# GpSimd rounds and subtracts the weight chunks up to the mixing weights in eight pieces each in place of four

## The chip, the cores and the metric

The kernel runs on one core of a Trainium2 chip. The metric is the device time of one launch in microseconds (us); lower is better. Before the change it is 1716.6 us, the median of three runs (1716.49 to 1716.98).

## What is computed

One decoder layer in float32 on a sequence of 1024 tokens with 1024 features: an input projection; for eight heads, sparse attention in which an indexer picks 256 keys for each query; for eight more heads, attention in a window of 128 tokens with learned sinks; an output projection; cross-attention into 256 memory tokens; an MLP of width 4096 with squared ReLU; a layer norm after each of the three parts.

```python
proj = h @ w_in[l] + b_in[l]
o_dsa = dsa_sparse_attention(dq, dk, dv, iq, ik, iw)      # top-256 keys by an indexer's score
o_swa = swa_sink_attention(sq, sk, sv, swa_sinks[l])
mix = jnp.concatenate([o_dsa, o_swa], axis=-1) @ w_o[l]
h = layer_norm(DEEPNORM_ALPHA * h + mix, ln1_g[l], ln1_b[l])
c = memory_cross_attention(h, mem, wq_mem[l], wk_mem[l], wv_mem[l], wo_mem[l])
h = layer_norm(DEEPNORM_ALPHA * h + c, ln2_g[l], ln2_b[l])
m = squared_relu_mlp(h, w_up[l], w_down[l])
h = layer_norm(DEEPNORM_ALPHA * h + m, ln3_g[l], ln3_b[l])
```

## The kernel before, in words

**Split products.** TensorE multiplies numbers of the type fp32r, which keeps fewer bits than float32. To lose nothing the kernel splits every operand into a rounded part (`hi`) and the rest (`lo`), and each product is three matmuls: hi times hi, hi times lo, lo times hi (`exact`, L584 to L586).

**Weight chunks.** All weights come as 68 chunks of 128 partitions by 2048 columns (chunk 0 has 1600 columns). Their order is fixed: 0 for the values and the indexer's weights (`C_V`), 1 for the keys, 2 to 7 for the queries, 8 to 23 for the four memory heads (four chunks a head: wk, wv, wq, wo), 24 to 27 for the mixing weights w_o, 28 to 35 for the two products of the cross-attention, 36 to 67 for the MLP. `C_MIX` is 24 and `C_G` is 28. SyncE (SP) loads a chunk into one of two buffers `raw`. GpSimd (POOL) then runs two passes over it: L570 rounds (`w_hi`, one input), L575 subtracts (`w_lo`, two inputs). Each pass is cut into `PIECES` instructions of equal width, four of 512 columns, with all rounding ahead of all subtracting. Each subtraction adds one to the semaphore `w_ready`. TensorE waits until all pieces of the chunk that it needs are counted, and SP until all pieces of the chunk two back are counted; nobody waits for a single piece. Up to chunk 23 there are two buffers for the split weights, so POOL starts a chunk once TensorE has used the chunk two back (`chunk_used`).

**The start.** VectorE (DVE) makes the angles for the rotary tables (L1114 to L1126, 1024 columns each, every one waiting for the one before), and then the lo parts of x (`x_lo`, L1130, eight of 1024 columns). ScalarE (ACT) rounds x (L864) and evaluates sine and cosine in between. TensorE's first matmul waits for chunk 0 and for the first `x_lo`.

**The middle.** TensorE projects the queries and keys (`project`), computes the indexer's scores, and then walks through the attention units, windowed heads first, with one product of the memory heads' weights (`memory_product`) put in after about every third unit of these. VectorE evacuates logits (L1465) and meanwhile finds each query's 256 best keys by a search over the bits of a threshold (`select_keys`): a counting pass over the scores (L1245, 384 to 768 columns), then three instructions of one to three columns each that take the bit back or keep it (L1287, L1293, L1299). ScalarE counts for the two widest tiles, and VectorE evaluates these counts (`set_wide`: L1378, L1383, L1389, L1397). All this is written in one fixed order for each engine.

**The rest.** From the last attention units on, TensorE has products to do almost without a break: mixing, cross-attention, MLP.

Of the kernel before, what the change touches and what calls it, by code (L numbers as in the profile page):

```python
# [55 lines left out]

V_COLS = HEADS + HEAD + 2 * HEAD
CHUNK = 2048
PIECES = 4
C_V, C_K, C_IQ, C_SQ, C_DQ = 0, 1, 2, 4, 6  # L60
C_MEM = 8
C_MIX = C_MEM + 4 * MEM_HEADS
C_G = C_MIX + 4
C_U = C_G + 4
C_MLP = C_U + 4
N_FF = FF // 256
N_CHUNKS = C_MLP + 2 * N_FF

TWO_PI = 2.0 * np.pi

# [119 lines left out]
def build_layer(nc, a):  # L190
# [6 lines left out]
    with ctx:  # L197
        def sem(name):
            return ctx.enter_context(nc.semaphore(name))
# [181 lines left out]
        w_rounded = sem("w_rounded")  # L381
        w_ready = sem("w_ready")
# [40 lines left out]
        def columns_of(c):  # L423
            return NK * V_COLS if c == C_V else CHUNK
# [21 lines left out]
        def _(sp):  # L446
# [58 lines left out]
            att_loaded = 3  # L505
            for c in range(2, N_CHUNKS):
                if c == C_DQ:
                    load_keys()
                    for j in range(NT - FIRST_TOPK_TILE):
                        load_queries(j)  # L510
                if c == C_MEM:
                    for j in range(3):
                        load_queries(NT - FIRST_TOPK_TILE + j)
                if c == C_MEM + 2:

                    chunk_used(sp, C_MEM - 1)
                    sp.dma_start(mem_raw[:], a["mem_t"]).then_inc(mem_in, 16)

                if C_MEM + 2 < c <= C_MIX + 2:
                    ahead = 2 * NT if c == C_MIX + 2 else 3 + (mem_unit(c - 3) - 1) // HEADS  # L520
                    while att_loaded < ahead:
                        load_queries(NT - FIRST_TOPK_TILE + att_loaded)
                        att_loaded += 1
                if c == C_MIX + 2:

                    chunk_used(sp, C_MIX - 1)
                    for s in range(2):
                        sp.wait_ge(stored[s], 16 * 4 * MEM_HEADS)

                    attended(sp, 2 * NT - 1)  # L530
                    load_gb(0)
                if c == C_U + 1:

                    sp.wait_ge(ln_done, NT)
                    load_gb(1)
                if c == C_MLP + 2:

                    sp.wait_ge(ln_done, 2 * NT)
                    load_gb(2)

                sp.wait_ge(w_ready, PIECES * (c - 1))
                dst = raw[c % 2][:, 0:columns_of(c)]
                if C_G <= c < C_MLP:
                    dst = dst.rearrange("p (k n) -> p k n", k=4)
                sp.dma_start(dst, source_of(c)).then_inc(raw_in[c % 2], 16)
# [7 lines left out]
        @block.gpsimd  # L553
        def _(pool):
            for c in range(N_CHUNKS):
                s, n = slot_of(c), columns_of(c)

                pool.wait_ge(raw_in[c % 2], 16 * (c // 2 + 1))

                if 2 <= c < C_MIX + 2:  # L560
                    chunk_used(pool, c - 2)
                elif C_MIX + 2 <= c < C_MIX + 4:

                    attended(pool, 2 * NT - 1)
                elif c >= C_MIX + 4:
                    chunk_used(pool, c - 4)

                for p in range(PIECES):
                    col = slice(p * n // PIECES, (p + 1) * n // PIECES)
                    pool.tensor_scalar(w_hi[s][:, col], raw[c % 2][:, col], 1.0, 1.0, ALU.mult, ALU.mult)\  # L570
                        .then_inc(w_rounded, 1)
                for p in range(PIECES):
                    col = slice(p * n // PIECES, (p + 1) * n // PIECES)
                    pool.wait_ge(w_rounded, PIECES * c + p + 1)
                    pool.tensor_tensor(w_lo[s][:, col], raw[c % 2][:, col], w_hi[s][:, col].bitcast(F32),  # L575
                                       ALU.subtract).then_inc(w_ready, 1)

# [2 lines left out]
        def _(pe):  # L580
# [11 lines left out]
                return [w[s][:, 0:n].rearrange("p (k n) -> p k n", k=k) for w in (w_hi, w_lo)]  # L592


            pe.wait_ge(w_ready, PIECES * (C_V + 1))
            wh, wl = parts_of(C_V, NK)
            for k in range(NK):
                pe.wait_ge(x_lo_done, k + 1)
# [7 lines left out]
            def project(r, j):  # L606

                c, _, hf = ROPE[r]
                n = A_ROPE + 2 * r + j
                if n == 0:  # L610

                    pe.wait_ge(v_done, 2)
                if r == N_ROPE_FIRST and j == 0:

                    indexed(pe, i_free, len(IDX) - 4)
                pe.wait_ge(w_ready, PIECES * (c + 1))
                freed(pe, a_free, n)
                wh, wl = parts_of(c, NK)
                col = slice(j * P, (j + 1) * P)
                tok = slice(hf * HALF, (hf + 1) * HALF)  # L620
                exact(ring_a[n % 2][:], [(wh[:, k, col], wl[:, k, col], x_hi[:, k, tok], x_lo[:, k, tok])
                                         for k in range(NK)]).then_inc(a_full[n % 2], 1)
# [30 lines left out]
            def memory_product(use):  # L653


                h, what = divmod(use, 10)
                n = A_MEM + 10 * h
                m = n + what
                if use == 0:
                    pe.wait_ge(mem_lo_done, 1)  # L660
                pe.wait_ge(w_ready, PIECES * (C_MEM + 4 * h + (what if what < 2 else 2 + (what - 2) // 4) + 1))
                freed(pe, a_free, m)
                dst = ring_a[m % 2]
                if what < 2:
                    wh, wl = parts_of(C_MEM + 4 * h + what, NK)
                    for j in range(2):
                        col = slice(j * P, (j + 1) * P)
                        mm = exact(dst[:, j * MEM:(j + 1) * MEM],
                                   [(wh[:, k, col], wl[:, k, col], mem_hi[:, k, :], mem_lo[:, k, :])
                                    for k in range(NK)])  # L670
                elif what < 6:

                    emptied(pe, a_free, n)
                    wh, wl = parts_of(C_MEM + 4 * h + 2, 2)
                    for j in range(2):
                        col = slice((2 * (what - 2) + j) * P, (2 * (what - 2) + j + 1) * P)
                        mm = exact(dst[:, j * MEM:(j + 1) * MEM],
                                   [(wh[:, k, col], wl[:, k, col], kv_hi[0][:, k, :], kv_lo[0][:, k, :])
                                    for k in range(2)])
                else:  # L680

                    emptied(pe, a_free, n + 1)
                    wh, wl = parts_of(C_MEM + 4 * h + 3, 2)
                    mt, half = divmod(what - 6, 2)
                    row = slice(mt * P, (mt + 1) * P)
                    col = slice(half * HALF, (half + 1) * HALF)
                    mm = exact(dst[:], [(kv_hi[1][:, k, row], kv_lo[1][:, k, row], wh[:, k, col], wl[:, k, col])
                                        for k in range(2)])
                mm.then_inc(a_full[m % 2], 1)
# [89 lines left out]
            def product(g):  # L779

                stage, ch, t = g // (2 * NT), g // NT % 2, g % NT
                n = L_GEMM + g
                c = C_MIX + 4 * stage + 2 * ch
                pe.wait_ge(w_ready, PIECES * (c + 2))
                act_split(stage, t)
                freed(pe, l_free, n)
                for kh in range(2):
                    wh, wl = parts_of(c + kh, 4)
                    mm = exact(ring_l[n % 2][:, 0:HALF],
                               [(act_hi[:, t, 4 * kh + k, :], act_lo[:, t, 4 * kh + k, :],  # L790
                                 wh[:, k, :], wl[:, k, :]) for k in range(4)],
                               first=(kh == 0), final=(kh == 1))
                mm.then_inc(l_full[n % 2], 1)

            def up(u):

                f, hf = divmod(u, 2)
                wh, wl = parts_of(C_MLP + 2 * f, NK)
                pe.wait_ge(w_ready, PIECES * (C_MLP + 2 * f + 1))
                if f == 0:  # L800
                    for t in range(4 * hf, 4 * hf + 4):
                        act_split(3, t)
                for j in range(2):
                    n = A_UP + 2 * u + j
                    freed(pe, a_free, n)
                    col = slice(j * P, (j + 1) * P)
# [5 lines left out]
            def down(u):  # L812

                f = u // 2
                wh, wl = parts_of(C_MLP + 2 * f + 1, 2)
                pe.wait_ge(w_ready, PIECES * (C_MLP + 2 * f + 2))

                pe.wait_ge(hid_ready, 2 * u + 2)
                for tt in range(4):
                    n = L_DOWN + 4 * u + tt  # L820
                    freed(pe, l_free, n)
                    tok = slice(tt * P, (tt + 1) * P)
                    for half in range(2):
                        col = slice(half * HALF, (half + 1) * HALF)
# [912 lines left out]
```

## Time and profile before

| | us |
|---|---|
| median of 3 runs | 1716.6 |
| the profiled execution's own time | 1712.85 |
| its span, first instruction to last | 1711.1 |
| TensorE busy | 1546.0 (90%) |
| VectorE busy | 965.3 (56%) |
| GpSimd busy | 551.4 (32%) |
| ScalarE busy | 443.5 (26%) |

The chain of waits that ended last is 72% TensorE, 19% VectorE, 3% ScalarE and 2% GpSimd; 4% is issue. Busy time includes the time in which an instruction has begun and is held up, so a short instruction with a long duration is one that waited inside its engine.

### The profile page before, as it was taken

To read this page: it belongs to the slowest core of one execution; us is meant where nothing else is said; L and a number is where in the kernel's file an instruction comes from. 1 tells how busy PE (TensorE), PEld (TensorE's weight loads), DVE (VectorE), ACT (ScalarE), POOL (GpSimd) and SP (SyncE) were. 2 spreads that over 40 slices of the span, in tenths; PEclk is the share of its full clock that TensorE was granted. 3 is DMA by queue.
4 is the path that set the end of the run, shared out by engine and by line. 5 is a ranking of instruction groups with operands and counts; after the bars stand their busy time and mean duration, and the time that the engine had idled before them with its cause. 6 is when DMAs were issued, how large, how long until landed. Compare 5 with 4: busy or idle time off the path is not lost.

```text
span 1711.1 us, 20895 instructions
## 1 busy us (share of the span) xinstructions
PE 1546.0 (90%) x7720; PEld 1305.8 (76%) x7720; DVE 965.3 (56%) x1819; ACT 443.5 (26%) x961; POOL 551.4 (32%) x548
## 2 busy tenths in 40 slices
PE   5997884688787999998999999999999999999993
PEld 5885663678686998877888778888888888888882
DVE  5568998799987443277442943333333333333348
ACT  2015334455544764112220111111111111111110
POOL 5341031364462000334333053333333333333100
PEclk9999997788886999999999999999999999999997
DMA  5463043243431102222110041111111111110002
GB/s 214 136 204 129 25 154 129 80 137 130 148 123 46 42 2 87 93 93 74 50 50 1 1 148 49 50 50 50 50 50 49 50 49 50 49 50 25 1 1 98
DMA packets 61332, 128.97 MB, mean 75 GB/s; under 512 B 6960, under 2 KB 34096, under 8 KB 53552
## 3 DMA queue, kind: packets, MB, share of 16 engines
q1 hardware_dynamic: 44208, 100.37, 17.5%
q10 hardware_dynamic: 17024, 27.27, 4.5%
q8 instruction: 62, 1.02, 0.2%
q14 instruction: 38, 0.31, 0.1%
HBM read 100.35 MB, written 27.26 MB: 75 GB/s over the span
## 4 chain that ended last, share of the span: by engine, by line
PE 72%; DVE 19%; issue 4%; ACT 3%; POOL 2%; ACTq 0%; DMA 0%; DVEq 0%; SPq 0%; POOLq 0%
PE banks L584 21%; PE banks L586 21%; PE banks L585 21%; PE banks L741 4%; DVE unread L1245 3%; PE banks L719 2%; DVE score L1216 2%; DVE h_buf L1546 1%; PE banks L751 1%; PE banks L633 1%; DVE bn L1532 1%; PE banks L634 1%; POOL w_lo L575 1%; ACT unread_wide L908 1%; DVE trial L1293 1%
## 5 line engine op out<-in xcount | busy, mean ns | idle before, releaser
L570 POOL TENSOR_SCALAR w_hi<-raw 128x512 fp32r<-128x512 f32 (+1 forms) x272 | 181.4, 693 | 1059.1 <-PE banks L586 770.2
L575 POOL TENSOR_TENSOR w_lo<-raw,w_hi 128x512 fp32r<-128x512 f32 (+1 forms) x272 | 372.5, 1400 | 0.0
L1657 DVE TENSOR_TENSOR h_buf<-h_buf,banks 128x1024 f32<-128x1024 f32 x120 | 146.4, 1220 | 146.6 <-PE banks L586 146.6
L584 PE MATMUL banks<-w_hi,hid_hi 128*128 128x512 f32 x512 | 200.8, 392 | 7.8 <-DVE h_buf L1657 7.8
L584 PE MATMUL banks<-act_hi,w_hi 128*128 128x512 f32 x512 | 200.1, 391 | 1.7 <-DVE act_lo L1525 1.7
L586 PE MATMUL banks<-w_hi,hid_lo 128*128 128x512 f32 x512 | 200.4, 391 | 0.0
L585 PE MATMUL banks<-w_lo,hid_hi 128*128 128x512 f32 x512 | 200.4, 391 | 0.0
L586 PE MATMUL banks<-act_hi,w_lo 128*128 128x512 f32 x512 | 199.9, 390 | 0.0
L585 PE MATMUL banks<-act_lo,w_hi 128*128 128x512 f32 x512 | 199.7, 390 | 0.0
L1621 DVE TENSOR_TENSOR relu_buf<-relu_buf 128x512 f32<-128x512 f32 x64 | 45.8, 716 | 248.3 <-ACT relu_buf L1071 248.3
L1071 ACT ACTIVATE relu_buf<-banks 128x512 f32<-128x512 f32 x64 | 38.3, 598 | 548.9 <-PE banks L586 548.9
L584 PE MATMUL banks<-w_hi,act_hi 128*128 128x512 f32 x384 | 152.6, 397 | 0.0
L586 PE MATMUL banks<-w_hi,act_lo 128*128 128x512 f32 x384 | 150.2, 391 | 0.0
L585 PE MATMUL banks<-w_lo,act_hi 128*128 128x512 f32 x384 | 149.9, 390 | 0.0
L633 PE MATMUL banks<-key_hi,q_tile 128*128 128x512 f32 (+3 forms) x240 | 96.0, 400 | 55.2 <-DVE neg_max L1465 25.4
L584 PEld LDWEIGHTS banks<-w_hi,hid_hi 128*128 128x128 f32 x512 | 96.8, 189 | 29.8 <-DVE h_buf L1657 7.0
L741 PE MATMUL banks<-v_all,prob_t 128*128 128x64 f32 x816 | 116.7, 284 | 0.0
L584 PEld LDWEIGHTS banks<-act_hi,w_hi 128*128 128x128 f32 x512 | 96.5, 188 | 22.1 <-issue 2.1
L741 PEld LDWEIGHTS banks<-v_all,prob_t 128*128 128x128 f32 x816 | 111.1, 207 | 1.7
L586 PEld LDWEIGHTS banks<-w_hi,hid_lo 128*128 128x128 f32 x512 | 96.8, 189 | 20.2
L585 PEld LDWEIGHTS banks<-w_lo,hid_hi 128*128 128x128 f32 x512 | 96.8, 189 | 20.0
L585 PEld LDWEIGHTS banks<-act_lo,w_hi 128*128 128x128 f32 x512 | 96.5, 189 | 20.1
(170 smaller groups left out, 2842.7 us busy)
## 6 DMA issues: line engine op xcount, KB each, us to landing
raw<-w_up_dram SPq DMA_DIRECT2D x16, 1024.0 KB, 4.9
raw<-w_down_dram SPq DMA_DIRECT2D x16, 1024.0 KB, 4.8
q_tile<-qk_dram SPq DMA_DIRECT2D x176, 64.0 KB, 2.1
qk_dram<-q_hi ACTq DMA_DIRECT2D x28, 256.0 KB, 2.1
qk_dram<-roped ACTq DMA_DIRECT2D x28, 256.0 KB, 2.5
x_raw<-x_t_dram SPq DMA_DIRECT2D x8, 512.0 KB, 9.1
raw<-wk_mem_dram SPq DMA_DIRECT2D x4, 1024.0 KB, 5.3
raw<-wv_mem_dram SPq DMA_DIRECT2D x4, 1024.0 KB, 5.1
```

The source lines that it names most:

```text
L570: pool.tensor_scalar(w_hi[s][:, col], raw[c % 2][:, col], 1.0, 1.0, ALU.mult, ALU.mult)\
L575: pool.tensor_tensor(w_lo[s][:, col], raw[c % 2][:, col], w_hi[s][:, col].bitcast(F32), ALU.subtract).then_inc(w_ready, 1)
L584: pe.matmul(dst, lh, rh, start=(first and n == 0), stop=False)
L585: pe.matmul(dst, lh, rl, start=False, stop=False)
L586: last = pe.matmul(dst, ll, rh, start=False, stop=(final and n == len(parts) - 1))
L633: pe.matmul(dst[:, lo:hi], q, key_hi[key][:, k0 + lo:k0 + hi], start=True, stop=False)
L719: mm = pe.transpose(ring_t[m % 2][:, (j % 4) * P:(j % 4 + 1) * P], prob[n % 2][:, j * P:(j + 1) * P], ident[:])
L741: mm = pe.matmul(dst[:, h * HEAD:(h + 1) * HEAD], prob_t[n % 2][:, j * P:(j + 1) * P], v_all[:, k0 + j, v0:v0 + HEAD], start=(j == 0), sto ...
L1071: act.activation(relu_buf[q % 2][:], ring_a[(A_UP + q) % 2][:], ACT.Relu)\
L1245: written.append(then(dve.tensor_scalar(dst, score[i][:], limit, start, compare, ALU.add, accum_out=count[:, c:c + 1])))
L1621: dve.tensor_tensor(relu_buf[q % 2][:], relu_buf[q % 2][:], relu_buf[q % 2][:], ALU.mult)\
L1657: dve.tensor_tensor(h_buf[:, t, :], h_buf[:, t, :], ring_l[n % 2][:], ALU.add)\
```

## The change

Chunks below `C_G` are cut into eight pieces instead of four: 256 columns each, and 200 in chunk 0. By the value of `C_G` these are chunks 0 to 27: the 24 up to the mixing weights, and the four of the mixing weights too. The counts that the engines wait for follow (`pieces_through`).

```diff
-PIECES = 4
+PIECES_EARLY, PIECES_LATE = 8, 4
+def pieces_of(c):
+    return PIECES_EARLY if c < C_G else PIECES_LATE
+def pieces_through(c):
+    return sum(pieces_of(b) for b in range(c + 1))
...
-                for p in range(PIECES):
-                    col = slice(p * n // PIECES, (p + 1) * n // PIECES)
+                for p in range(pieces_of(c)):
+                    col = slice(p * n // pieces_of(c), (p + 1) * n // pieces_of(c))
                     pool.tensor_scalar(w_hi[s][:, col], raw[c % 2][:, col], 1.0, 1.0, ALU.mult, ALU.mult)\
                         .then_inc(w_rounded, 1)
...
-                    pool.wait_ge(w_rounded, PIECES * c + p + 1)
+                    pool.wait_ge(w_rounded, pieces_through(c - 1) + p + 1)
                     pool.tensor_tensor(w_lo[s][:, col], raw[c % 2][:, col], w_hi[s][:, col].bitcast(F32),
                                        ALU.subtract).then_inc(w_ready, 1)
...
-            pe.wait_ge(w_ready, PIECES * (C_V + 1))
+            pe.wait_ge(w_ready, pieces_through(C_V))
```

On GpSimd, chunks 0 and 1 stand like this before (`raw_49` and `raw_50` are the two load buffers, `w_hi_51` and `w_lo_55` the first pair of split buffers, `_52` and `_56` the second):

```order
L570 TENSOR_SCALAR w_hi_51<-raw_49 128x400 [waits raw_in0]
L570 TENSOR_SCALAR w_hi_51<-raw_49 128x400 x3
L575 TENSOR_TENSOR w_lo_55<-raw_49,w_hi_51 128x400 [waits w_rounded] x4
L570 TENSOR_SCALAR w_hi_52<-raw_50 128x512 [waits raw_in1]
L570 TENSOR_SCALAR w_hi_52<-raw_50 128x512 x3
L575 TENSOR_TENSOR w_lo_56<-raw_50,w_hi_52 128x512 [waits w_rounded] x4
```

And now, at the same place on GpSimd:

```order
L582 TENSOR_SCALAR w_hi_51<-raw_49 128x200 [waits raw_in0]
L582 TENSOR_SCALAR w_hi_51<-raw_49 128x200 x7
L587 TENSOR_TENSOR w_lo_55<-raw_49,w_hi_51 128x200 [waits w_rounded] x8
L582 TENSOR_SCALAR w_hi_52<-raw_50 128x256 [waits raw_in1]
L582 TENSOR_SCALAR w_hi_52<-raw_50 128x256 x7
L587 TENSOR_TENSOR w_lo_56<-raw_50,w_hi_52 128x256 [waits w_rounded] x8
```

The columns and their order are the same and the instructions twice as many. What the passes wait for, and the order on every other engine, is as before.

## Rows read from the trace of the kernel before

**Rows 1.** Windows: us, busy us of each engine (instructions), PEclk, DMA share, GB/s.
```profile
19.67:131.58 111.91, 111.91 (x576) 96.55 (x576) 60.66 (x74) 12.71 (x19) 46.09 (x40) 1.00 0.49 159
...
400.00:500.00 100.00, 79.77 (x522) 73.96 (x520) 95.64 (x249) 49.78 (x131) 60.55 (x60) 0.88 0.40 130
```

**Rows 2.** Chain of waits at the start: start us, us, what.
```profile
19.67 0.53 PE banks L584
```

**Rows 3.** Timeline, GpSimd in chunk 0: start us, us, instruction, count.
```profile
8.95 1.49 POOL L570 TENSOR_SCALAR w_hi<-raw 128x400 fp32r<-128x400 f32 x1
10.40 1.49 POOL L570 TENSOR_SCALAR w_hi<-raw 128x400 fp32r<-128x400 f32 x1
...
14.20 2.00 POOL L575 TENSOR_TENSOR w_lo<-raw,w_hi 128x400 fp32r<-128x400 f32 x1
16.16 1.48 POOL L575 TENSOR_TENSOR w_lo<-raw,w_hi 128x400 fp32r<-128x400 f32 x1
```

**Rows 4.** Timeline, VectorE and ScalarE beside it.
```profile
7.37 4.14 DVE L1119 SCALAR_TENSOR_TENSOR angle<-turns,angle 128x1024 f32<-128x1024 f32 x3
11.54 0.90 DVE L1121 TENSOR_SCALAR angle<-angle 128x1024 f32<-128x1024 f32 x1
12.47 0.88 DVE L1124 TENSOR_SCALAR turns<-angle 128x1024 f32<-128x1024 f32 x1
...
16.81 12.36 DVE L1130 TENSOR_TENSOR x_lo<-x_raw,x_hi 128x1024 fp32r<-128x1024 f32 x8
...
16.78 1.06 ACT L870 ACTIVATE cos<-turns 128x1024 f32<-128x1024 f32 x1 [3.25 <-DVE turns L1126]
17.75 5.77 ACT L864 ACTIVATE x_hi<-x_raw 128x1024 fp32r<-128x1024 f32 x6
```

**Rows 5.** Timeline, GpSimd in chunk 1.
```profile
23.42 1.58 POOL L570 TENSOR_SCALAR w_hi<-raw 128x512 fp32r<-128x512 f32 x1
...
28.06 2.25 POOL L575 TENSOR_TENSOR w_lo<-raw,w_hi 128x512 fp32r<-128x512 f32 x1
30.27 1.28 POOL L575 TENSOR_TENSOR w_lo<-raw,w_hi 128x512 fp32r<-128x512 f32 x1
```

**Rows 6.** Timeline, GpSimd in chunk 18 and the first of 19.
```profile
422.66 2.37 POOL L570 TENSOR_SCALAR w_hi<-raw 128x512 fp32r<-128x512 f32 x4 [1.79 <-PE banks L586]
424.99 5.03 POOL L575 TENSOR_TENSOR w_lo<-raw,w_hi 128x512 fp32r<-128x512 f32 x4
429.99 2.37 POOL L570 TENSOR_SCALAR w_hi<-raw 128x512 fp32r<-128x512 f32 x4
```

**Rows 7.** Timeline, TensorE's first matmul with chunks 10, 18 and 22.
```profile
327.25 0.38 PE L584 MATMUL banks<-kv_hi,w_hi 128*128 128x256 f32 x1 [0.63 <-POOL w_lo L575]
...
430.08 0.39 PE L584 MATMUL banks<-kv_hi,w_hi 128*128 128x256 f32 x1
...
487.24 0.58 PE L584 MATMUL banks<-kv_hi,w_hi 128*128 128x256 f32 x1 [2.07 <-POOL w_lo L575]
```

**Rows 8.** Timeline, VectorE beside chunk 12; then line L1293: min/median/max ns.
```profile
348.47 1.20 DVE L1293 TENSOR_TENSOR trial<-refused,trial_next 128x3 int32<-128x3 int32 x1
349.70 1.23 DVE L1299 TENSOR_SCALAR trial_next<-trial 128x3 int32<-128x3 int32 x1
...
L1293 DVE TENSOR_TENSOR trial<-refused,trial_next x60: 146/162/1330, 216.2 to 457.4; 128x3 int32<-128x3 int32 x30, 128x1 int32<-128x1 int32 x30
```

**Rows 9.** Groups of VectorE, 160 to 514 us: count | busy us, mean ns | idle.
```profile
L1293 DVE TENSOR_TENSOR trial<-refused,trial_next 128x3 int32<-128x3 int32 (+1 forms) x60 | 22.5, 375 | 1.0
L1299 DVE TENSOR_SCALAR trial_next<-trial 128x3 int32<-128x3 int32 (+1 forms) x58 | 18.7, 322 | 1.0
L1287 DVE TENSOR_SCALAR refused<-count 128x3 int32<-128x3 f32 (+1 forms) x62 | 13.4, 216 | 0.0
...
L1389 DVE TENSOR_TENSOR trial<-refused,trial_next 128x2 int32<-128x2 int32 x30 | 10.3, 344 | 1.0
L1383 DVE TENSOR_SCALAR refused<-level 128x2 int32<-128x2 f32 x31 | 10.2, 328 | 0.6
```

More of the change, by code:

```diff
@@ L539, in _ @@
                     load_gb(2)
-                sp.wait_ge(w_ready, PIECES * (c - 1))
+                sp.wait_ge(w_ready, pieces_through(c - 2))
                 dst = raw[c % 2][:, 0:columns_of(c)]
@@ L566, in _ @@
                     chunk_used(pool, c - 4)
-                for p in range(PIECES):
-                    col = slice(p * n // PIECES, (p + 1) * n // PIECES)
+                for p in range(pieces_of(c)):
+                    col = slice(p * n // pieces_of(c), (p + 1) * n // pieces_of(c))
                     pool.tensor_scalar(w_hi[s][:, col], raw[c % 2][:, col], 1.0, 1.0, ALU.mult, ALU.mult)\
                         .then_inc(w_rounded, 1)
-                for p in range(PIECES):
-                    col = slice(p * n // PIECES, (p + 1) * n // PIECES)
-                    pool.wait_ge(w_rounded, PIECES * c + p + 1)
+                for p in range(pieces_of(c)):
+                    col = slice(p * n // pieces_of(c), (p + 1) * n // pieces_of(c))
+                    pool.wait_ge(w_rounded, pieces_through(c - 1) + p + 1)
                     pool.tensor_tensor(w_lo[s][:, col], raw[c % 2][:, col], w_hi[s][:, col].bitcast(F32),
@@ L615, in project @@
                     indexed(pe, i_free, len(IDX) - 4)
-                pe.wait_ge(w_ready, PIECES * (c + 1))
+                pe.wait_ge(w_ready, pieces_through(c))
                 freed(pe, a_free, n)
@@ L660, in memory_product @@
                     pe.wait_ge(mem_lo_done, 1)
-                pe.wait_ge(w_ready, PIECES * (C_MEM + 4 * h + (what if what < 2 else 2 + (what - 2) // 4) + 1))
+                pe.wait_ge(w_ready, pieces_through(C_MEM + 4 * h + (what if what < 2 else 2 + (what - 2) // 4)))
                 freed(pe, a_free, m)
@@ L783, in product @@
                 c = C_MIX + 4 * stage + 2 * ch
-                pe.wait_ge(w_ready, PIECES * (c + 2))
+                pe.wait_ge(w_ready, pieces_through(c + 1))
                 act_split(stage, t)
@@ L798, in up @@
                 wh, wl = parts_of(C_MLP + 2 * f, NK)
-                pe.wait_ge(w_ready, PIECES * (C_MLP + 2 * f + 1))
+                pe.wait_ge(w_ready, pieces_through(C_MLP + 2 * f))
                 if f == 0:
@@ L815, in down @@
                 wh, wl = parts_of(C_MLP + 2 * f + 1, 2)
-                pe.wait_ge(w_ready, PIECES * (C_MLP + 2 * f + 2))
+                pe.wait_ge(w_ready, pieces_through(C_MLP + 2 * f + 1))
                 pe.wait_ge(hid_ready, 2 * u + 2)
```

## The prediction, made before the changed kernel was run

> **What bounds the kernel now.** I read the chain of waits first: it is TensorE nearly all the way, except for the first 20 us and for about 130 to 545 us, where VectorE leads. Then the windows. From 19.67 to 131.58 us TensorE is busy for the whole 111.91 us, so whatever moves its start moves everything behind; from 400 to 500 us VectorE is busy 95.64 of 100 us, TensorE 79.77 [rows 1]. The change touches GpSimd between 7.6 and 697 us, so three things are to be read from the timeline: when TensorE gets its first weights, where TensorE waits for a chunk in the middle, and what GpSimd's instructions do to VectorE beside them.
>
> TensorE's first matmul starts at 19.67 us [rows 2], right behind the last piece of chunk 0.
>
> **What a piece costs.** Undisturbed, four roundings of 512 columns take 424.99 - 422.66 = 2.33 us, 0.583 each from start to start, and four subtractions 429.99 - 424.99 = 5.00 us, 1.25 each [rows 6]. No piece of 256 columns is in the trace, but two widths are. Beside VectorE's instructions of 1024 columns, roundings of 400 columns start 10.40 - 8.95 = 1.45 us apart [rows 3], those of 512 (28.06 - 23.42) / 3 = 1.547 us apart [rows 5]: 0.09 us for 112 columns, 0.84 ns a column. Subtractions: 16.16 - 14.20 = 1.96 us [rows 3] against 30.27 - 28.06 = 2.21 us [rows 5], 2.2 ns a column. So 256 columns less make a rounding 0.215 us shorter (0.37) and a subtraction 0.56 us shorter (0.69). Two halves cost 0.15 and 0.13 us more than the whole. Bounds: nothing (cost goes with columns) and a doubling (cost by instruction). I take the slope. A chunk alone is then 4 x 0.28 = 1.1 to 1.2 us longer, about 8.5 us in place of 7.33.
>
> The Trainium skill (GPSIMD Engine Reference, Performance versus the Vector engine) gives a two-input operation of 2048 columns 4497 ns; with the row of 1.25 us for 512 that is an estimate of 2.1 ns a column, near this slope, and leaves the sum as it is.
>
> **How the two engines meet.** In chunk 0 the pieces and VectorE's instructions take turns, one for one. A rounding lasts 1.49 us [rows 3], far over the 0.58 us of a wider one alone [rows 6], and VectorE's angle instructions of one input take 0.90 and 0.88 us [rows 4]. In the search, L1293 with three columns takes 1.20 us and L1299 behind it 1.23 us, each about one subtraction, where the median is 0.162 us [rows 8]. Each engine is held until the other's instruction in progress is over. The Trainium skill has this as a rule (SBUF — State Buffer, Who interferes with whom): the pair of ports that both share is locked for a whole instruction, and a VectorE instruction with two SBUF inputs, or with one in a two-port mode, contends. By that rule the number of pieces decides how often each engine is held, and the length how long; it cuts both ways here, as the next two terms show.
>
> **Term 1, the start: +8.0 us.** In chunk 0, GpSimd has 8 pieces of 400 columns and ends at 19.62; four roundings and four subtractions met seven VectorE instructions. With 16 pieces it meets more. From the end of VectorE's first angle instruction, about 8.60 us (7.37 us [rows 4] plus a third of the group, unhindered), I go turn by turn. A turn with a 1024-column instruction of two inputs is 1.455 us for a rounding of 400 columns, less 200 x 0.84 ns: 1.287. With an angle instruction of one input a turn was 12.47 - 11.54 = 0.93 us [rows 4] and becomes 0.76. Eight roundings meet two L1119, L1121, L1124, L1125, L1126 and two x_lo: 5 x 1.287 + 3 x 0.76 = 8.7, to 17.3 us. Then six subtractions meet the six other x_lo: 1.965 - 200 x 2.14 ns = 1.54 each, 9.2 us, to 26.5; the last two run alone, 0.5 and 0.6, to 27.6. The same count with the old turns (1.44 for the subtraction of 1.48 us that met L1126 [rows 3], less the 0.04 us by which two rows overlap; 0.90 for the last, which meets nothing new) is 2 x 1.455 + 2 x 0.93 + 1.965 + 1.44 + 1.965 + 0.90 = 11.04, from 8.60 to 19.64, where the trace has 19.67 for TensorE [rows 2]. Is VectorE always ready for its turn? ScalarE's cosine waits for L1126, which ends near 14.8 here; six more x_hi follow at 5.77 / 6 = 0.96 us each [rows 4], faster than turns of 1.54, and the first is there at about 16.9, before VectorE asks. So TensorE starts 27.6 - 19.6 = 8.0 us later. It has no gap up to 131.58 us, and what it then works on has no other source, so all 8.0 us pass to the end. Chunk 1 ends near 36 us, before TensorE wants it (about 52). Lower bound: no more turns than before, only the longer work, +1.2. I take 8.0, since the old turns add up to the trace.
>
> **Term 2, chunks that TensorE waits for: +4 us.** Chunk 10: idle 0.63 us before 327.25; chunk 22: 2.07 us before 487.24; chunk 18 is ready when TensorE comes, at 430.08 [rows 7], its last piece having ended near 430.02 [rows 6]. All three start right behind TensorE's use of the chunk two back, so each hands on 1.2 us: 3.5. In chunk 22 VectorE's wide instructions alternate with the pieces as at the start, and one more may fall in: 0.6. The next closest, chunks 13, 14, 17 and 21, are ready 2.3 to 3.6 us before they are needed; 1.2 us more is hidden there, and the cover stays unless VectorE's gain also brings the need forward. Chunks 24 to 27 have over 30 us. Range 1.2 to 6.
>
> **Term 3, shorter holds in the search: -10 us.** From 160 to 514 us, over 0.16 us each (0.15 for L1287), the five groups of [rows 9] lost 60 x 0.213 + 58 x 0.16 + 62 x 0.066 + 30 x 0.184 + 31 x 0.168 = 12.8 + 9.3 + 4.1 + 5.5 + 5.2 = 37 us; with L1378, L1184 and smaller ones I put it at 46 us. 19 chunks are split there, 2.4 us lost in each, beside 7.33 - 2.4 = 4.9 us of VectorE's own work. A hold shrinks from 1.25 to 0.69 us, by 0.55; but the window is 8.5 us long, so it catches more instructions. Per us of own work the loss falls from 0.49 to 0.27, so own work in the window is 8.5 / 1.27 = 6.7 and the loss 1.8: 0.6 us gained a chunk, 11 us in 19. About a tenth of it falls where TensorE leads anyway: 10. Upper bound: every hold shrinks and nothing more is caught, 0.45 x 46 = 20 less what is off the chain, about 17. Lower bound 0: two engines that always take turns lose the whole length of the pieces, however they are cut. I take 10, since VectorE's counting passes (over half of its time) are not held and so break the turns.
>
> **Sum.** 8.0 + 4 - 10 = +2: span 1713.1 from 1711.1 and the profiled execution's 1712.85 to about 1714.9. The runs' median is 3.75 us above that execution's own time; the same stands above here: 1716.6 + 2.1 = 1718.7 us. A change under 0.2% (3.4 us) can't be told from none.
>
> **Rivals.**
> *A, the gain is handed back (slower).* The instruction that escapes early runs into the next piece. In the window from 346 to 353 us the sequence L1378, L1383, L1389 stands at its end; a longer window catches all three where now only the first is held. If that is the rule, the gain is 2 to 5 us, and 8 + 4 - 4 = +8: 1724.6. It turns slower when the gain is below 8.6 us. For it: 16% more time in windows. Against: the holds of 1.20 and 1.23 us stand in pairs, and each piece is halved.
> *B, the start does not take turns (faster).* If VectorE, coming back sooner after short pieces, keeps its place and GpSimd is held no oftener, term 1 is +1.2 and the sum 1.2 + 4 - 10 = -5: 1712. Against it: the turn-by-turn sum hits 19.64.
> *C, the gain is whole (faster).* 17 us gained: 8 + 4 - 17 = -5: 1712. For it: 46 us are lost now. Against: the catch above.
> *D, nothing on any path:* against it, TensorE's first wait ends with chunk 0's last piece.
>
> **How the numbers follow.** Forecast 0.50 (1715.5 to 1722), A 0.28, B 0.10, C 0.10, D 0.02. Forecast splits 0.38 within 0.2% and 0.12 slower; A gives 0.26 slower and 0.02 same; B and C 0.18 faster and 0.02 same; D same. Faster 0.18, same 0.44, slower 0.38. Range 1711 to 1725.5: it leaves out the ends of A, B and C.
>
> **What would show it.** First matmul at 27.6 us (B: near 21). Roundings of 256 columns alone 0.37 us apart, subtractions 0.69. L1293 held 0.6 to 0.7 us where it was 1.20. First use of chunk 10 with an idle of about 1.8 us before it. The time from the first matmul to the last attention product 6 us shorter than before (A: as long or longer; C: 13 shorter). A first matmul at 20 us, or pieces of 256 as long as those of 512, would make the prediction wrong in its base.

## The result: 8 us slower, and the profile after

| | before | after |
|---|---|---|
| median of 20 runs each, us | 1715.71 | 1723.78 |
| lowest to highest | 1713.35 to 1717.18 | 1713.72 to 1732.28 |
| the profiled execution's own time | 1712.85 | 1718.93 |
| its span | 1711.1 | 1717.1 |

The ratio of after to before is 1.0048, with a 95% interval of 1.0033 to 1.0063: about 8 us slower. The prediction said 1718.7, and no change as the likeliest. The time lies in its range, but 5 us above the point, and at rival A's figure. The spread is new as well: 18.6 us where the kernel before has 3.8. The profiled execution is one of the quicker ones, 4.9 us under the median, so its trace shows less than what a usual run loses.

**The start.** The chain of waits of the changed kernel, from GpSimd's two passes over chunk 0 to TensorE's first matmuls (start us, us, what):

```profile
7.38 7.78 POOL w_hi L582 x8
15.16 12.38 POOL w_lo L587 x8
27.58 0.53 PE banks L596
28.12 0.21 PE banks L597
```

TensorE starts at 27.58 us in place of 19.67 [rows 2]. The landing of chunk 0 moves this by up to 1.3 us from trace to trace; from GpSimd's first piece to the first matmul it is 20.2 us in each of the three traces with eight pieces in chunk 0 (this one, runs 1 and 8) and 12.0 to 12.5 us in the ten with four. In the timeline VectorE beside it, where every instruction takes turns with a piece, as in [rows 4]:

```profile
7.39 3.99 DVE L1131 SCALAR_TENSOR_TENSOR angle<-turns,angle 128x1024 f32<-128x1024 f32 x3
11.42 0.73 DVE L1133 TENSOR_SCALAR angle<-angle 128x1024 f32<-128x1024 f32 x1
12.18 0.72 DVE L1136 TENSOR_SCALAR turns<-angle 128x1024 f32<-128x1024 f32 x1
...
15.01 12.06 DVE L1142 TENSOR_TENSOR x_lo<-x_raw,x_hi 128x1024 fp32r<-128x1024 f32 x8
```

A turn with the one-input L1133 is 12.18 - 11.42 = 0.76 us long. Windows of the changed kernel over the same two stretches as [rows 1]:

```profile
27.58:138.09 110.51, 110.50 (x576) 95.20 (x576) 44.14 (x67) 8.86 (x14) 48.09 (x80) 1.00 0.48 158
...
400.00:500.00 100.00, 76.45 (x505) 70.44 (x504) 89.25 (x253) 46.76 (x122) 69.36 (x122) 0.90 0.38 124
```

The first projections take 110.51 us instead of 111.91, so in this trace 1.4 of the 7.9 us come back at once. That is not a gain of the change: the same stretch takes 112.04 and 111.59 us in the traces of runs 1 and 8, which also have eight pieces in chunk 0 (the last section says why it varies). Between 400 and 500 us both engines do less than before: TensorE 76.45 (79.77), VectorE 89.25 (95.64). GpSimd is the busier one, 69.36 (49.78).

**A chunk alone.** GpSimd in chunk 18 and the first pass of 19, timeline, against [rows 6]:

```profile
425.01 2.99 POOL L582 TENSOR_SCALAR w_hi<-raw 128x256 fp32r<-128x256 f32 x8 [1.73 <-PE banks L598]
427.97 5.58 POOL L587 TENSOR_TENSOR w_lo<-raw,w_hi 128x256 fp32r<-128x256 f32 x8
433.53 2.99 POOL L582 TENSOR_SCALAR w_hi<-raw 128x256 fp32r<-128x256 f32 x8
```

Roundings start 2.96 / 8 = 0.37 us apart and subtractions 5.56 / 8 = 0.70. The chunk takes 8.52 us in place of 7.33.

**Chunks that TensorE waits for.** Its first matmuls with chunks 10, 18 and 22, timeline, against [rows 7]:

```profile
332.95 0.39 PE L596 MATMUL banks<-kv_hi,w_hi 128*128 128x256 f32 x1 [1.80 <-POOL w_lo L587]
...
433.60 0.39 PE L596 MATMUL banks<-kv_hi,w_hi 128*128 128x256 f32 x1 [1.24 <-POOL w_lo L587]
...
495.95 0.58 PE L596 MATMUL banks<-kv_hi,w_hi 128*128 128x256 f32 x1 [4.75 <-POOL w_lo L587]
```

Chunks 14 and 21 are now waited for as well, 1.26 and 1.10 us. The five waits come to 10.2 us, where the trace of before has 0.63 + 0.08 + 2.07 = 2.8: 7.4 us more.

**The search.** Groups of VectorE from 160 to 514 us (count | busy us, mean ns | idle), against [rows 9]; the last line is L1390, which was L1378 before:

```profile
L1305 DVE TENSOR_TENSOR trial<-refused,trial_next 128x3 int32<-128x3 int32 (+1 forms) x60 | 15.1, 252 | 1.0
L1299 DVE TENSOR_SCALAR refused<-count 128x3 int32<-128x3 f32 (+1 forms) x62 | 12.2, 197 | 0.0
L1311 DVE TENSOR_SCALAR trial_next<-trial 128x3 int32<-128x3 int32 (+1 forms) x58 | 11.3, 195 | 1.0
L1401 DVE TENSOR_TENSOR trial<-refused,trial_next 128x2 int32<-128x2 int32 x30 | 9.2, 306 | 1.0
L1395 DVE TENSOR_SCALAR refused<-level 128x2 int32<-128x2 f32 x30 | 9.1, 304 | 0.5
L1390 DVE TENSOR_TENSOR level<-count,offset 128x2 f32<-128x2 f32 x30 | 21.7, 723 | 4.9 <-ACT banks L920 4.8
```

The first five groups lost as the prediction wanted, and more: 22.5 - 15.1 = 7.4, 18.7 - 11.3 = 7.4, 13.4 - 12.2 = 1.2, and 1.1 and 0.8 in the last two (one instruction fewer is in the records): 17.9 us. The sixth gave 13 of it back. The same group in the kernel before:

```profile
L1378 DVE TENSOR_TENSOR level<-count,offset 128x2 f32<-128x2 f32 x31 | 8.5, 274 | 4.4 <-ACT banks L908 4.3
```

The line view of the changed kernel (ns, min/median/max) says that this isn't a shift of all instructions but one or a few of them:

```profile
L1390 DVE TENSOR_TENSOR level<-count,offset x31: 149/161/8178, 220.3 to 516.8; 128x2 f32<-128x2 f32 x31
```

VectorE's timeline around that one, which is to be laid beside GpSimd's rows of chunk 19 above (433.53, and its last subtraction ends at 442.00):

```profile
432.86 1.06 DVE L1257 TENSOR_SCALAR_CACHE_REDUCE unread<-score,trial,minus_rank 128x768 uint8<-128x768 f32 x1
433.85 0.08 DVE L1257 DVE_READ_ACCUMULATOR unread<-score,trial,minus_rank 128x1 f32 x1
433.85 8.18 DVE L1390 TENSOR_TENSOR level<-count,offset 128x2 f32<-128x2 f32 x1
441.95 0.15 DVE L1299 TENSOR_SCALAR refused<-count 128x3 int32<-128x3 f32 x1
```

A subtraction of two columns, with a median of 0.161 us, is held 8.18 us: over all sixteen pieces of chunk 19, until GpSimd stops. Two more are held over seven and over three pieces (4.25 us from 337.16, 1.93 us from 390.96), again to the last piece of their chunk. I call a hold over more than two pieces a long hold. The trace of before has none: every hold there ends with one piece.

### The profile page after: what moved, and what is told of

The parts are those of the page before. It is cut to its first block, busy times and chain, and to the rows that moved or that the text cites. A ratio compares the mean times of both kernels' runs of the same rounds, so it can differ in the third digit from the quotient of the medians.

```text
span 1717.1 us, 21119 instructions
## 1 busy us (share of the span) xinstructions
PE 1539.9 (90%) x7720; PEld 1299.0 (76%) x7720; DVE 948.1 (55%) x1819; ACT 443.1 (26%) x961; POOL 591.8 (34%) x772
## 4 chain that ended last, share of the span: by engine, by line
PE 72%; DVE 19%; issue 3%; POOL 3%; ACT 2%; ACTq 0%; DMA 0%; DVEq 0%; SPq 0%; POOLq 0%
PE banks L596 21%; PE banks L598 20%; PE banks L597 20%; PE banks L753 4%; DVE unread L1257 3%; PE banks L731 2%; DVE score L1228 2%; POOL w_lo L587 2%; PE banks L645 1%; DVE h_buf L1558 1%; PE banks L763 1%; POOL w_hi L582 1%; PE banks L646 1%; DVE bn L1544 1%; DVE level L1390 1%
## 5 line engine op out<-in xcount | busy, mean ns | idle before, releaser
L582 POOL TENSOR_SCALAR w_hi<-raw 128x256 fp32r<-128x256 f32 (+2 forms) x384 | 204.4, 562 | 1025.1 <-PE banks L598 746.4
L587 POOL TENSOR_TENSOR w_lo<-raw,w_hi 128x256 fp32r<-128x256 f32 (+2 forms) x384 | 390.0, 1050 | 0.0
L598 PEld LDWEIGHTS banks<-act_hi,w_lo 128*128 128x128 f32 x512 | 96.1, 188 | 20.0
```

The source lines that it names most:

```text
L598: last = pe.matmul(dst, ll, rh, start=False, stop=(final and n == len(parts) - 1))
```

## The experiments

Each ran in five rounds beside the kernel before, whose medians in the three batches were 1716.21 (the first four runs), 1714.67 (the next four) and 1716.01 (the last four). Ratios are to the kernel before. 1% is 17.2 us, and an interval of a ratio is about 2 us to each side, wider in runs 2 and 7.

**1. Only chunk 0 in eight pieces.**

```diff
-    return PIECES_EARLY if c < C_G else PIECES_LATE
+    return PIECES_EARLY if c == 0 else PIECES_LATE
```

> Chunk 0 alone in eight pieces, every other chunk in four. Turn-taking at the start: first matmul near 27.6 us instead of 19.67, and the time +6.5 to +8 us against before, less if TensorE is sooner at full speed. Rival (the loss comes from the middle, where chunks 10, 14, 18, 21 and 22 are waited for): within 1.5 us of before.

Measured: 1722.39 us, ratio 1.0036 (1.0024 to 1.0048), 6 us slower. First matmul at 27.43 us, no long hold. The start's loss is real and reaches the end: nothing else differs, and this trace's first projections give nothing back.

**2. All but chunk 0.**

```diff
+    return PIECES_EARLY if 0 < c < C_G else PIECES_LATE
```

> Chunks 1 to 27 in eight pieces, chunk 0 in four. If the start is the whole loss and the middle pays for itself: first matmul at 19.6 us and the time 0 to 2 us from before (the trace of the changed kernel is 7.9 us late at the first matmul and 6.0 us at the end). If the forecast of -10 for the search and +4 for the waits held: -6. Rival, the gain of the search is handed back and the waits grow: +2 to +5.

Measured: 1715.94 us (1707.41 to 1725.51), ratio 1.0005 (0.9988 to 1.0022). First matmul at 19.65 us. So all that the pieces do behind the start comes to nothing on the average, and it carries the spread of 18 us. Its trace has four long holds (8.52, 4.83, 8.18 and 3.42 us). The longest, from its timeline, VectorE and then GpSimd:

```profile
324.97 0.08 DVE L1257 DVE_READ_ACCUMULATOR unread<-score,trial,minus_rank 128x1 f32 x1
324.97 8.52 DVE L1299 TENSOR_SCALAR refused<-count 128x3 int32<-128x3 f32 x1
333.52 0.16 DVE L1305 TENSOR_TENSOR trial<-refused,trial_next 128x3 int32<-128x3 int32 x1
```

```profile
324.96 3.00 POOL L582 TENSOR_SCALAR w_hi<-raw 128x256 fp32r<-128x256 f32 x8
327.92 5.54 POOL L587 TENSOR_TENSOR w_lo<-raw,w_hi 128x256 fp32r<-128x256 f32 x8
```

Again sixteen pieces, from the first to the last of a chunk; and another instruction than in the changed kernel (L1299, not L1390), so the line is not the cause.

**3. Eight pieces only where TensorE does not wait.**

```diff
+    return PIECES_EARLY if 0 < c < C_G and c not in (10, 14, 18, 21, 22) else PIECES_LATE
```

> Eight pieces in chunks 1 to 27 except 10, 14, 18, 21 and 22, which TensorE waits for; these and chunk 0 in four. Theory that shorter pieces free VectorE in the search: -4 to -10 us against before. Rival, the escaping instruction only runs into the next piece and the longer window eats the gain: within 1.5 us of before.

Measured: 1704.03 us, ratio 0.9934 (0.9923 to 0.9946), 11 to 12 us faster than before. The idle before chunks 10, 14, 18, 21 and 22 is 0.64, 0.07, 0.08, 0 and 0.96 us. One long hold, of 5.38 us, on a line that is no part of the search:

```profile
L1504 DVE TENSOR_TENSOR sums<-sums,sink_exp x8: 160/325/5380, 328.1 to 530.1; 128x8 f32<-128x8 f32 x8
```

**4. Only the five waited-for chunks in eight.**

```diff
+    return PIECES_EARLY if c in (10, 14, 18, 21, 22) else PIECES_LATE
```

> Eight pieces in chunks 10, 14, 18, 21 and 22 alone. Theory that TensorE's waits for a chunk grow by the longer work: in the changed kernel's trace these five waits sum to 10.2 us against 2.8 before, so +3.6 (1.2 us for each of 10, 18 and 22) to +7 us. Rival, VectorE's gain beside them pays for it: within 1.5 us of before.

Measured: 1721.29 us (1716.87 to 1725.22), ratio 1.0027 (1.0017 to 1.0037). Idle of 1.80, 1.23, 0.86 and 4.75 us before 10, 18, 21 and 22. A piece of 512 columns doesn't protect: in chunk 11, which has four of them and a start right behind chunk 10, an instruction of VectorE was held over all eight instructions; two more long holds stand in chunks 19 (4.44 us, pieces of 512) and 14 (1.89 us, pieces of 256). The line view has the longest:

```profile
L1299 DVE TENSOR_SCALAR refused<-count x62: 138/152/7331, 215.5 to 470.2; 128x3 int32<-128x3 f32 x31, 128x1 int32<-128x1 f32 x31
```

**5. Chunk 0 in two pieces.**

```diff
+    return 2 if c == 0 else PIECES_LATE
```

> Chunk 0 in two pieces of 800 columns, every other chunk in four. Turn-taking: with four instructions GpSimd meets three of VectorE's and is through near 16.2 us, but VectorE is held 0.7 us by each rounding and 1.75 by each subtraction, so that the first x_lo ends near 20.0; TensorE then waits for x_lo and starts at about 20.0, no sooner than before (19.67), and the time is within 1.5 us of before. Rival, the start goes with the number of pieces alone (four pieces 19.6, eight 27.6): first matmul near 16 us, 3.5 us faster.

Measured: 1715.72 us, ratio 1.0005 (0.9997 to 1.0014); first matmul at 20.22 us. The limit moved to the other side of the same exchange of turns, as the chain of waits shows: VectorE's angle instructions now wait out pieces of 800 columns (L1133, below, the first subtraction), and TensorE waits for VectorE's first `x_lo`.

```profile
12.28 2.25 DVE angle L1133
...
18.85 1.24 DVE x_lo L1142
20.09 0.14 issue
20.22 0.51 PE banks L596
```

**6. Two pieces in twelve chunks of the search.**

```diff
+    return 2 if c in (7, 8, 9, 11, 12, 13, 15, 16, 17, 19, 20, 23) else PIECES_LATE
```

> Two pieces of 1024 columns in chunks 7, 8, 9, 11, 12, 13, 15, 16, 17, 19, 20 and 23, every other chunk in four. If the gain of eight pieces there (12 us) comes from shorter holds of VectorE's small instructions, longer ones must lose: a small instruction beside a subtraction held up to 2.3 us, and +5 to +12 us against before. Rival (what counts is how often VectorE is held, or something else in that version): the same or faster than before.

Measured: 1725.61 us, ratio 1.0058 (1.0046 to 1.007), some 10 us slower. No long hold, but VectorE is held by pieces of 2.3 us (timeline beside chunk 11):

```profile
331.55 2.28 DVE L1305 TENSOR_TENSOR trial<-refused,trial_next 128x3 int32<-128x3 int32 x1
333.86 2.31 DVE L1311 TENSOR_SCALAR trial_next<-trial 128x3 int32<-128x3 int32 x1
```

The length of a piece counts, then, in the direction that term 3 said.

**7. Sixteen pieces of 128 columns in ten chunks.**

```diff
+    if c in (7, 8, 9, 11, 12, 15, 16, 19, 20, 23):
+        return 16
+    return PIECES_EARLY if 0 < c < C_G and c not in (10, 14, 18, 21, 22) else PIECES_LATE
```

> Sixteen pieces of 128 columns in chunks 7, 8, 9, 11, 12, 15, 16, 19, 20 and 23, which TensorE needs more than 6 us after they are ready; eight in the others that are not waited for; four in 0, 10, 14, 18, 21 and 22. Holds of about 0.42 us in place of 0.69: 2 to 4 us faster than eight pieces there (-14 to -16 against before) if the holds' length is what counts. Rival, a chunk of nearly 11 us catches more instructions and more long holds: slower than eight pieces there.

Measured: 1725.29 us (1717.41 to 1734.93), ratio 1.0079 (1.0052 to 1.0106). My theory was wrong here and the rival right. If only the length of a piece counted, this would be the fastest; it is among the slowest, with seven long holds in its trace. Five are of 2 to 8 us and like those above; the line views show the longest of each group (lines here are two further down than in the changed kernel):

```profile
L1301 DVE TENSOR_SCALAR refused<-count x62: 138/153/8327, 215.0 to 470.3; 128x3 int32<-128x3 f32 x31, 128x1 int32<-128x1 f32 x31
...
L1307 DVE TENSOR_TENSOR trial<-refused,trial_next x60: 142/163/5990, 215.2 to 465.7; 128x3 int32<-128x3 int32 x30, 128x1 int32<-128x1 int32 x30
```

The two others are of another kind. In chunk 8 a VectorE instruction of 512 columns, whose shortest takes 0.69 us, is held over all sixteen subtractions, and no read of an accumulator stands before it. In chunk 11 one of eight columns is held over five roundings and is through at 329.08 us, before GpSimd's last rounding, which ends at 329.24 us (timelines):

```profile
246.83 0.74 DVE L1183 SCALAR_TENSOR_TENSOR rot_part<-banks,bias_qk,sin 128x512 f32<-128x512 f32 x1
247.60 7.23 DVE L1187 TENSOR_TENSOR roped<-roped,rot_part 128x512 f32<-128x512 f32 x1
...
247.65 6.64 POOL L589 TENSOR_TENSOR w_lo<-raw,w_hi 128x128 fp32r<-128x128 f32 x16
...
327.79 1.29 DVE L1506 TENSOR_TENSOR sums<-sums,sink_exp 128x8 f32<-128x8 f32 x1
```

The theory that the rest tests was put on record together with run 7: a long hold needs GpSimd to issue piece upon piece, and a stop between pieces ends it.

**8. The changed kernel with stops.** In chunks 11, 15, 19 and 23 GpSimd waits until its last instruction is complete before it issues the next.

```diff
+                    if c in (11, 15, 19, 23):
+                        pool.wait_ge(w_rounded, pieces_through(c - 1) + p)
+                        if p == 0:
+                            pool.wait_ge(w_ready, pieces_through(c - 1))
                     pool.tensor_scalar(w_hi[s][:, col], ...)
...
+                    if c in (11, 15, 19, 23) and p:
+                        pool.wait_ge(w_ready, pieces_through(c - 1) + p)
                     pool.tensor_tensor(w_lo[s][:, col], ...)
```

> The changed kernel, but in chunks 11, 15, 19 and 23 GpSimd waits for each of its pieces to be complete before it starts the next. In the changed kernel's trace three short VectorE instructions there are held 4.25, 1.93 and 8.18 us, across up to 16 pieces and until GpSimd's run of pieces ends. Theory that back-to-back pieces never let them in: with a full stop between pieces no hold is longer than one piece (0.75 us), and the time is 6 to 12 us shorter than the changed kernel's (near 1712 to 1718) with less spread from run to run. Rival (the long holds have another cause, or cost nothing on the path): holds of several us remain, or the time stays near 1724.

Measured: 1707.78 us (1706.46 to 1710.44), ratio 0.9965 (0.9953 to 0.9977): 14 us less than the changed kernel by the ratios, 16 by the medians, and the spread is down to 4 us. The waits cost GpSimd 2.3 us in each of chunks 11, 15 and 19 (10.8 in place of 8.5), more in chunk 23. At the same place as the hold of 8.18 us, its timeline has (lines six further down):

```profile
431.42 3.81 POOL L586 TENSOR_SCALAR w_hi<-raw 128x256 fp32r<-128x256 f32 x8 [0.18 <-POOL w_lo L593]
435.31 6.87 POOL L593 TENSOR_TENSOR w_lo<-raw,w_hi 128x256 fp32r<-128x256 f32 x8
```

```profile
431.54 0.08 DVE L1263 DVE_READ_ACCUMULATOR unread<-score,trial,minus_rank 128x1 f32 x1
431.54 0.29 DVE L1396 TENSOR_TENSOR level<-count,offset 128x2 f32<-128x2 f32 x1
431.75 0.15 DVE L1305 TENSOR_SCALAR refused<-count 128x3 int32<-128x3 f32 x1
```

**9 to 12. Stops with other pieces.** The stops of run 8 are in all four; what differs is the function of the pieces.

```diff
 # 9: as run 3
+    return PIECES_EARLY if 0 < c < C_G and c not in (10, 14, 18, 21, 22) else PIECES_LATE
 # 10: as before the change
+    return PIECES_LATE
 # 11: as run 2
+    return PIECES_EARLY if 0 < c < C_G else PIECES_LATE
 # 12: as 9, with a case of its own
+    if c in (10, 14, 18, 21, 22):
+        return 2
```

> Eight pieces in chunks 1 to 27 except 10, 14, 18, 21 and 22, which stay at four like chunk 0; in chunks 11, 15, 19 and 23 GpSimd waits for each piece's completion before the next. Theory (the long holds that end with GpSimd's back-to-back run are what eats the gain, and completion waits take them away): no hold of VectorE over more than one piece in 11, 15, 19, 23, first matmul near 19.7 us, idle before chunk 10 near 0.6 and before 14 and 21 near 0. Time at or under the same kernel without the stops (1704.0): 1697 to 1703, ratio to the kernel before about 0.989 to 0.993. Rival (the stops in the changed kernel helped by another way, such as moving the later chunks against VectorE's work): no gain over 1704, 1704 to 1710, since here the chunks that could move have four pieces.

> The kernel before (four pieces everywhere) with the stops alone, in chunks 11, 15, 19 and 23. Theory (stops pay by removing long holds, and four pieces of 512 mostly have none): within 2 us of the kernel before, 1713 to 1717, holds of 1.2 to 1.3 us as before. Rival (the stops are themselves the gain, because VectorE gets in at every stop): 5 us or more faster than the kernel before, under 1710.

> Chunk 0 in four pieces, 1 to 27 in eight, with the stops in 11, 15, 19, 23. Theory (the costs are independent: the start 6.2 us, the long holds about 14 to 16): the changed kernel with stops (1707.8) less 6.2, about 1701.6 (1699 to 1704); first matmul near 19.7 us; idle of 1.8, 1.2, 1.2 and over 4 us before chunks 10, 14, 18 and 22. Rival (the start's loss is swallowed later, so it matters only where nothing else waits): 1706 or more.

> As the kernel with eight pieces outside the waited-for chunks and with stops, but chunks 10, 14, 18, 21 and 22 in two pieces of 1024 columns. By the cost of a piece (0.15 and 0.13 us for each cut) a chunk alone is 0.55 us shorter, so the idle before chunk 10 is near 0.1 and before 22 about 0.5 less: 1 to 1.5 us gained there. Against it, holds of up to 2.4 us in place of 1.25 in five chunks; two pieces in twelve chunks lost 11 us, 0.9 each, so up to 4.5 lost. Sum: 1 us faster to 3 us slower than the version with four there.

| | pieces | us (range) | ratio to before | same without stops |
|---|---|---|---|---|
| 9 | 8, waited-for chunks 4 | 1696.93 (1693.04 to 1697.82) | 0.9884 (0.9871 to 0.9897) | 0.9934 |
| 10 | 4 everywhere | 1711.33 (1707.39 to 1713.12) | 0.9970 (0.9958 to 0.9982) | 1 |
| 11 | 8, chunk 0 with 4 | 1700.05 (1699.04 to 1702.61) | 0.9909 (0.9896 to 0.9921) | 1.0005 |
| 12 | 8, waited-for chunks 2 | 1699.80 (1698.06 to 1700.92) | 0.9904 (0.9891 to 0.9917) | not run |

None of the four traces has a long hold. Run 9 is the fastest kernel of the study, 19 us or 1.2% under the kernel before, and just under the quick end of what the theory said. Run 11 came out as expected. TensorE's first matmul with chunks 10 and 22 in run 9 and then in run 11 (timelines):

```profile
324.51 0.39 PE L602 MATMUL banks<-kv_hi,w_hi 128*128 128x256 f32 x1 [0.64 <-POOL w_lo L593]
...
476.62 0.39 PE L602 MATMUL banks<-kv_hi,w_hi 128*128 128x256 f32 x1 [2.04 <-POOL w_lo L593]
```

```profile
325.67 0.39 PE L602 MATMUL banks<-kv_hi,w_hi 128*128 128x256 f32 x1 [1.82 <-POOL w_lo L593]
...
480.22 0.58 PE L602 MATMUL banks<-kv_hi,w_hi 128*128 128x256 f32 x1 [4.77 <-POOL w_lo L593]
```

Run 10 falls between the sides and nearer the rival: the stops alone, with pieces of 512, gain 5 us, where I expected under 2 and the rival 5 or more. Part of it shows in the traces: the ordinary holds come to 41.5 us in this one and to 44.2 in that of before (the table in the next section). For the rest, the kernel before may have long holds in executions that were not profiled (run 4 shows that pieces of 512 allow them); that stays open. Run 12 takes TensorE's waits for the five chunks away but for 0.05 us and is no faster than run 9; it is 3 us behind, with intervals that overlap. Its trace has ordinary holds of 34.9 us where run 9 has 29.3: pieces of 1024 columns hold VectorE for longer.

## Why the number was near and the mechanism was not

The time lies in the stated range, but that is in part luck: a loss of about 10 us that the prediction did not have was met by a gain in term 3 that was about 5 us larger than forecast.

**Term 1, the start, was right.** It said 27.6 us for the first matmul, the trace has 27.58. The length of a turn came as worked out, 0.76 us with a one-input instruction and 1.55 beside an `x_lo`; the count inside the sum did not. The roundings were over at 15.16 us, not 17.3, since two were done when VectorE's first angle instruction ended and none met an `x_lo`; the subtractions took 12.4 us, not 10.3, since all eight met an `x_lo`, not six. The two errors of 2.1 us cancel, so the hit to 0.02 us is luck, and what holds is that more pieces meet more of VectorE's instructions. The price in time, by three pairs that differ in chunk 0 alone: run 1 against before 1.0036 - 1 = 6.2 us, after against run 2 1.0048 - 1.0005 = 7.4, run 8 against run 11 0.9965 - 0.9909 = 9.6. The mean is 7.7, for 8.0 predicted. Rivals B and D fall with this.

**Term 2, the waits, named the right chunks and missed two.** The sum of idle grew by 7.4 us, not 4. Chunks 14 and 21 had been put down as hidden, unless VectorE's gain brought the need forward. For chunk 14 that fits: in run 4, with no gain elsewhere, TensorE doesn't wait for it. For chunk 21 it can't be all, since run 4 has a wait of 0.86 us there. In chunk 22, where VectorE's wide instructions take turns with the pieces, the wait grew by 2.7 us, not 1.2 + 0.6. The price in time is smaller than the idle: runs 11 and 9 differ in the five chunks alone, by 7.4 us of idle (1.82 + 1.29 + 1.26 + 1.08 + 4.77 against 0.64 + 0.07 + 0.06 + 0 + 2.04) and by 0.9909 - 0.9884 = 4.3 us of time. Two reasons are open to this, and no run parts them: VectorE leads in this stretch, and beside these five chunks too its holds get shorter. So the size of the term was right and its working was not.

**Term 3, shorter holds, was right as far as it went.** L1293 is down from a mean of 375 to 252 ns, and the five groups gained 17.9 us where I had about 11 in all and 10 on the path. In time: runs 9 and 10 have the same stops and the same waited-for chunks and differ in pieces of eight or four elsewhere, 0.9884 - 0.9970 = 14.8 us. The gain lies between the point and rival C. One reading behind the 10 was off: VectorE's counting passes are about 0.4 of its 322 busy us between 160 and 514 us, not over half.

**The step that failed is "Each engine is held until the other's instruction in progress is over."** It describes nearly all holds. The few that it doesn't cost nearly as much as the change gains. For the table, the rows of VectorE's instructions of up to eight columns that overlap a piece, between 160 and 520 us, are summed, each by its time above the shortest of its line, names and shape; the last row is the stretch in which the prediction wanted 6 us less.

| one trace each, us | before | after | run 2 | run 8 | run 9 | run 10 |
|---|---|---|---|---|---|---|
| ordinary holds | 44.2 | 28.3 | 25.5 | 30.8 | 29.3 | 41.5 |
| long holds | 0 | 13.9 | 24.4 | 0 | 0 | 0 |
| first matmul to last attention product | 653.3 | 650.3 | 657.0 | 639.3 | 637.1 | 651.3 |

The ordinary holds shrank by 16 us, and three long ones gave 14 of it back; the stretch came out 3 us shorter, not 6, of which 1.4 are those of the first projections.

In time, stops took 14.2 us off the changed kernel (1.0048 to 0.9965), 16.5 off run 2 (run 11), 8.6 off run 3 (run 9), but 5.1 off the kernel before (run 10). If a stop's other effects are worth those 5.1 us with pieces of 256 too, which is assumed, what the eight pieces add to the long holds is 14.2 - 5.1 or 16.5 - 5.1, 9 to 11 us. By the terms so measured: 7.7 + 4.3 - 14.8 + 10 = 7.2 us, against 8.2 from the ratio. This is no independent check, as the terms come from the same chain of runs that leads from before to after. With the first three terms alone the changed kernel would have been about 3 us faster, which a measurement just can't tell from no change.

The Trainium skill (SBUF — State Buffer, Who interferes with whom) has the pair of ports locked for a whole instruction. It doesn't say who gets the pair next when one engine issues instruction upon instruction; I took it that the waiting engine does, so that a hold can't outlast a piece. The row of 8178 ns over sixteen pieces shows that it can, and the measurement decides.

**Rival A** forecast 8 us slower and the number came out, but not by its mechanism. It let an instruction that escapes one piece run into the next, for a gain of 2 to 5 us. The ordinary holds in fact gained 15. The loss sits in three or four single instructions of 2 to 8 us, each held over many pieces, which neither it nor the forecast had.

**What decides on a long hold is open.** Shown: of the 18 in the 14 traces, 17 end with the last piece of a chunk, in one case (run 4, 383.52 us) with the next chunk's pieces right behind, and one, of 1.29 us in run 7, ends earlier; they don't depend on the line, nor on the width of the pieces (128, 256 and 512 columns all have them); and the traces with stops in chunks 11, 15, 19 and 23 have none. Why a stop ends them is not shown: a mere pause between pieces, without a wait for completion, was not tried. Of the 18, 16 stand right behind VectorE's read of its accumulator at the end of a counting pass or of a logits evacuation, as in the rows of 433.85 and 324.97 us. But in the changed kernel's trace 60 of the 140 instructions of up to eight columns beside pieces stand so, and 57 of them were held for one piece or not at all; that is a mark, not a cause. I did not try to move such a read away.

## What to carry to other kernels

Cutting a helper engine's instructions finer makes each hold of its neighbour shorter, but it costs a fixed time per instruction where somebody waits for the whole, and it adds turns where both engines are busy with wide instructions. So cut fine only where nobody waits for the end: that alone made a loss of 0.5% into a gain of 0.7%. Before summing holds by their mean, look at the longest of each group; if a short instruction is held over several of the helper's, let the helper wait for its own completion between them, which brought the gain to 1.2%.

## What was not expected of the hardware

Single instructions of VectorE, all but one of them short, were held over 3 to 23 consecutive instructions of GpSimd, 1.3 to 8.5 us, in 17 of 18 cases to the last piece of a chunk. The changed kernel's time spreads over 18.6 us from run to run, and over 4 us with the stops; but one long hold in a trace doesn't make a wide spread, as run 3 has one and spreads over 3 us.

At its start TensorE's matmuls come at half their later pace for a time that isn't fixed: every 0.21 us from 20.20 to 26.18 us before, from 28.12 to 31.32 us after, then every 0.11, with a granted clock of 1.00 in the windows of both. That shorter slow stretch makes the 1.4 us by which the first projections were quicker in the changed kernel's trace. In other traces it lasts between these two lengths or a little longer, whatever the pieces of chunk 0, so it isn't an effect of the change.
